# One ScalarE operation of 2048 columns for the hi part of a second-pass weight block, in place of two of 1024

## The chip, the cores and the metric

The kernel runs on one core of a Trainium2 chip. The metric is the device time of one launch in microseconds, as the median of several runs. The kernel before has a median of 2189.2 us over three runs (2186.03 to 2189.44).

## What is computed

One layer of an encoder over 512 tokens of width 2048, batch 1, all in float32: a normalisation, forgetting attention with 16 heads, a residual sum, a second normalisation and a SwiGLU feed-forward block of inner width 5632.

```python
def reference(x, ...):
    h = rmsnorm(x, mix_norm_g[0])
    x = x + forgetting_attention(h, fox_w_in[0], fox_b_f[0], fox_q_norm_g[0],
                                 fox_k_norm_g[0], fox_w_out[0])
    h = rmsnorm(x, ffn_norm_g[0])
    return x + swiglu(h, ffn_w_gate_up[0], ffn_w_down[0])

def swiglu(h, w_gu, w_down):
    gu = jnp.einsum('bsd,df->bsf', h, w_gu)
    gate, up = gu[..., :D_FF], gu[..., D_FF:]
    return jnp.einsum('bsf,fd->bsd', jax.nn.silu(gate) * up, w_down)
```

The change lies in the feed-forward block alone, in both of its matrix products (up: 2048 to 2 x 5632, down: 5632 to 2048).

## The kernel before

Every engine has its own program, written out by hand in one block each (`block.sync`, `block.gpsimd`, `block.tensor`, `block.scalar`, `block.vector`). An engine works through its program in order, and waits for others by semaphores that count up. Attention takes the first 834 us of the profiled execution, and the feed-forward block the rest.

**Products in hi and lo parts.** A float32 operand is split in two: ScalarE copies it in the narrower type that TensorE multiplies fast (`f_hi`), VectorE subtracts the copy from the original (`f_lo`), and TensorE makes each product of three matmuls (lines 723 to 725).

**Seven products in place of eight.** The feed-forward products are made by a Strassen-like scheme on 2 x 2 blocks, with seven block products. A *round* r makes one group of output columns (512 columns of each of two column blocks). Rounds 0 to 10 make the up product, rounds 11 to 16 the down product. A round has two *passes*, g = 0 and g = 1, and each pass has one *unit* per pair of blocks along the inner dimension: eight units in rounds 0 to 12, seven in rounds 13 to 16. All units, 264 of them, are numbered through by n (`UNITS`); so rounds 0 to 12 have 16 units each, and the second pass of round 2 is units 40 to 47.

- A first-pass unit loads three weight blocks of 128 x 512 (its raw buffer `f_raw` has four places of this size), and TensorE makes three products, 18 matmuls.
- A second-pass unit loads four blocks. VectorE turns them, in place, into four sums by three operations: t1 (line 1350, 1024 columns, gives places 0 and 1), then t2 (line 1355, gives place 3), then t3 (line 1357, gives place 2). Each adds one to the semaphore `t_step`; each of the later two waits for the one before. TensorE makes four products, 24 matmuls.

**The steps of a unit.** SyncE issues the load of unit n when TensorE is through with unit n - 4, since `f_raw` has four buffers. VectorE makes t1, t2, t3 of unit n + 2 while TensorE is in unit n. ScalarE makes `f_hi` of unit n + 2 (function `weights_hi`), which also waits for `unit_done`, that is until TensorE is through with unit n - 1, since `f_hi` has three buffers. For a second-pass unit it does so in two halves: line 1010 makes places 0 and 1 and waits for the first count of `t_step` only, and `weights_hi_rest`, line 1014, makes places 2 and 3 and waits for the third. VectorE then makes `f_lo` of the whole unit in one operation (`weights_lo`, line 1344), which waits for as many counts of `f_hi_done` as `HI_COUNT[n]` says. TensorE waits for `f_lo_done` at the start of each unit, and for nothing else in most.

**The order on VectorE.** In its iteration n of a second pass, VectorE issues t1(n + 2), then f_lo(n + 1), then t2(n + 2) and t3(n + 2). In two iterations of a round ("meeting": the last but one of the first pass, and the first of the second) f_lo comes ahead of t1. At the end of the first pass it reads product 2 out of PSUM (`read_p2`, line 1363, in the down rounds `add_p2_p3`, lines 1423 and 1428), at the end of the second the other products. In rounds 10 to 16 it also makes the lo parts of stored activations for the down product (`down_forms_lo`, line 1414), in many units at the end of the iteration.

**The order on ScalarE.** Beside `f_hi` it reads product 1 (`read_p1`, line 1027) and in the up rounds product 3 (`read_p3`, line 1034) out of PSUM at the last unit of the first pass. TensorE may write product 6 of the second pass only after product 1 has been read, and product 4 only after product 3 has been read; these are the second and the fourth product of the first second-pass unit.

## Time and profile before

| | |
|---|---|
| median of three runs | 2189.2 us (2186.03 to 2189.44) |
| profiled execution | 2189.52 us |
| its span | 2187.8 us |
| TensorE busy | 2129.5 us, 97% of the span |
| VectorE busy | 1524.6 us, 70% |
| ScalarE busy | 915.4 us, 42% |
| mean granted TensorE clock | 0.992 of full speed |

The span is the time from the first to the last instruction that was profiled; 1.7 us of the profiled execution lie outside it. Busy times of different engines overlap. A matmul of TensorE is recorded with 0.39 us, but the next one starts 0.23 us after it, as they are pipelined. On VectorE and ScalarE an operation that follows another without a wait starts some 0.1 us before the recorded end of the one before.

### The profile page before, as it was taken

The page shows a single profiled execution, that of the slowest core. Times are in us where ns is not written, and L with a number is a line of the kernel's source. Part 1 is how long each engine was busy: PE and PEld are TensorE (multiplying, and loading weights), DVE is VectorE, ACT ScalarE, POOL GpSimd, SP SyncE. Part 2 cuts the span into 40 slices and gives each one's busy share as a digit, 9 for nine tenths or more (in the row PEclk, how much of TensorE's full clock was granted, in tenths as well). Part 3 has the DMA queues.
Part 4 walks back from the last instruction along what each step waited for, and adds up shares of the span by engine and source line. Part 5 has one row for each costly group of instructions (what it writes and reads, how often), then busy time and mean ns, then how long its engine had stood idle before and what let it go on. Part 6 is the DMA issues. An engine that isn't in the chain of part 4 may idle for free.

```text
span 2187.8 us, 27845 instructions
## 1 busy us (share of the span) xinstructions
PE 2129.5 (97%) x10404; PEld 1852.7 (85%) x10404; DVE 1524.6 (70%) x2103; ACT 915.4 (42%) x1225; POOL 183.8 (8%) x356
## 2 busy tenths in 40 slices
PE   9999999999999999999999999999999989999997
PEld 8999999999998887888888888888887777777786
DVE  4544444444464445987888888788798888898888
ACT  5433333333343334444444444444445534444432
POOL 0322213222230000000000000000000001000000
PEclk9999999999999999999999999999999999999999
DMA  6332333333343335566566566567668757757755
GB/s 181 88 92 82 88 85 90 85 89 81 92 144 135 116 106 163 178 226 220 179 222 226 177 219 229 190 207 228 193 207 280 261 201 270 236 177 250 234 175 178
DMA packets 258331, 376.30 MB, mean 172 GB/s; under 512 B 15762, under 2 KB 114100, under 8 KB 257220
## 3 DMA queue, kind: packets, MB, share of 16 engines
q1 hardware_dynamic: 254864, 354.90, 51.6%
q10 hardware_dynamic: 3380, 20.21, 2.2%
q8 instruction: 58, 0.95, 0.2%
q14 instruction: 29, 0.24, 0.0%
HBM read 346.45 MB, written 28.61 MB: 171 GB/s over the span
## 4 chain that ended last, share of the span: by engine, by line
PE 83%; DVE 9%; DMA 6%; issue 1%; SPq 1%; POOL 0%; ACT 0%; DVEq 0%; POOLq 0%; ACTq 0%
PE gemm L522 11%; PE gemm L524 11%; PE gemm L523 11%; PE gemm L723 8%; PE gemm L725 8%; PE gemm L724 8%; PE aux L723 7%; PE aux L725 7%; PE aux L724 6%; DVE f_lo L1344 4%; DMA f_raw<-in_ffn_w_gate_up 3%; DMA f_raw<-in_ffn_w_down 2%; DVE f_raw L1350 2%; PE aux L523 1%; PE aux L524 1%; PE aux L522 1%
## 5 line engine op out<-in xcount | busy, mean ns | idle before, releaser
L1344 DVE TENSOR_TENSOR f_lo<-f_raw,f_hi 128x2048 fp32r<-128x2048 f32 (+1 forms) x264 | 534.2, 2030 | 63.9 <-ACT f_hi L1007 51.4
L522 PE MATMUL gemm<-w_hi,act_t 128*128 128x384 f32 (+2 forms) x1280 | 450.6, 352 | 1.6 <-DVE w_lo L1123 1.6
L524 PE MATMUL gemm<-w_hi,act_t 128*128 128x384 f32 (+2 forms) x1280 | 444.0, 347 | 0.0
L523 PE MATMUL gemm<-w_lo,act_t 128*128 128x384 f32 (+2 forms) x1280 | 443.9, 347 | 0.0
L723 PE MATMUL gemm<-f_hi,a_form 128*128 128x512 f32 x1056 | 412.4, 391 | 0.4 <-DVE rows L1428 0.4
L724 PE MATMUL gemm<-f_lo,a_form 128*128 128x512 f32 x1056 | 411.7, 390 | 0.0
L725 PE MATMUL gemm<-f_hi,a_form 128*128 128x512 f32 x1056 | 411.3, 389 | 0.0
L723 PE MATMUL aux<-f_hi,a_form 128*128 128x512 f32 x792 | 318.3, 402 | 42.8 <-DVE f_lo L1344 42.8
L725 PE MATMUL aux<-f_hi,a_form 128*128 128x512 f32 x792 | 312.2, 394 | 0.0
L724 PE MATMUL aux<-f_lo,a_form 128*128 128x512 f32 x792 | 311.9, 394 | 0.0
L1123 DVE TENSOR_TENSOR w_lo<-w_raw,w_hi 128x768 fp32r<-128x768 f32 (+1 forms) x160 | 160.8, 1009 | 208.5 <-ACT w_hi L818 208.5
L1007 ACT ACTIVATE f_hi<-f_raw 128x1536 fp32r<-128x1536 f32 x132 | 196.0, 1487 | 253.8 <-PE gemm L725 93.2
L522 PEld LDWEIGHTS gemm<-w_hi,act_t 128*128 128x128 f32 x1280 | 241.0, 188 | 12.4 <-issue 2.0
L523 PEld LDWEIGHTS gemm<-w_lo,act_t 128*128 128x128 f32 x1280 | 241.0, 188 | 10.4
L524 PEld LDWEIGHTS gemm<-w_hi,act_t 128*128 128x128 f32 x1280 | 240.8, 188 | 10.1
L723 PEld LDWEIGHTS gemm<-f_hi,a_form 128*128 128x128 f32 x1056 | 199.1, 189 | 42.6 <-DVE rows L1428 0.8
L724 PEld LDWEIGHTS gemm<-f_lo,a_form 128*128 128x128 f32 x1056 | 199.0, 188 | 41.6
L725 PEld LDWEIGHTS gemm<-f_hi,a_form 128*128 128x128 f32 x1056 | 198.8, 188 | 41.7
L1010 ACT ACTIVATE f_hi<-f_raw 128x1024 fp32r<-128x1024 f32 x132 | 139.9, 1060 | 222.2 <-DVE f_raw L1350 218.2
L1014 ACT ACTIVATE f_hi<-f_raw 128x1024 fp32r<-128x1024 f32 x132 | 140.2, 1062 | 210.5 <-DVE f_raw L1357 210.5
L723 PEld LDWEIGHTS aux<-f_hi,a_form 128*128 128x128 f32 x792 | 150.3, 190 | 88.2 <-DVE f_lo L1344 58.5
L818 ACT ACTIVATE w_hi<-w_raw 128x768 fp32r<-128x768 f32 (+1 forms) x160 | 136.4, 883 | 187.8 <-PE gemm L524 187.8
(161 smaller groups left out, 2143.0 us busy)
## 6 DMA issues: line engine op xcount, KB each, us to landing
f_raw<-in_ffn_w_gate_up SPq DMA_DIRECT2D x264, 512.0 KB, 4.2
f_raw<-in_ffn_w_down SPq DMA_DIRECT2D x132, 512.0 KB, 4.8
w_raw<-in_fox_w_in SPq DMA_DIRECT2D x192, 256.0 KB, 3.4
f_raw<-in_ffn_w_gate_up SPq DMA_DIRECT2D x88, 256.0 KB, 4.0
w_raw<-in_fox_w_out SPq DMA_DIRECT2D x16, 1024.0 KB, 5.1
a_raw<-forms_scratch SPq DMA_DIRECT2D x22, 512.0 KB, 6.3
f_raw<-in_ffn_w_down SPq DMA_DIRECT2D x44, 256.0 KB, 4.8
forms_scratch<-fa_a ACTq DMA_DIRECT2D x11, 896.0 KB, 6.3
```

Of the source, the lines that this page charges most:

```text
L522: mm(out, a_hi, b_hi, start=first, stop=False)
L523: mm(out, a_hi, b_lo, start=False, stop=False)
L524: return mm(out, a_lo, b_hi, start=False, stop=last)
L723: mm(banks[t][:], st_hi, hi, start=j == 0, stop=False)
L724: mm(banks[t][:], st_hi, lo, start=False, stop=False)
L725: i = mm(banks[t][:], st_lo, hi, start=False, stop=j == ROUND_K[r] - 1)
L818: a.activation(w_hi[:, j % 2, k, 0:width], w_raw[:, j % 2, k, 0:width], ACT.Copy)\
L1007: a.activation(f_hi[:, n % 3, 0:3], f_raw[:, n % 4, 0:3], ACT.Copy).then_inc(f_hi_done, 1)
L1010: a.activation(f_hi[:, n % 3, 0:2], f_raw[:, n % 4, 0:2], ACT.Copy).then_inc(f_hi_done, 1)
L1014: a.activation(f_hi[:, n % 3, 2:4], f_raw[:, n % 4, 2:4], ACT.Copy).then_inc(f_hi_done, 1)
L1123: v.tensor_tensor(w_lo[:, j % 2, k, 0:width], w_raw[:, j % 2, k, 0:width], f32(w_hi[:, j % 2, k, 0:width]), ALU.subtract).then_inc(w_lo_do ...
L1344: v.tensor_tensor(f_lo[:, n % 4, 0:3 + g], f_raw[:, n % 4, 0:3 + g], f32(f_hi[:, n % 3, 0:3 + g]), ALU.subtract).then_inc(f_lo_done, 1)
```

## The change

`weights_hi` makes the four places of a second-pass unit in one operation of 2048 columns. It waits for the third count of `t_step`, as the second half did. `weights_hi_rest` is gone, and with it one count of `f_hi_done` for each of the 132 second-pass units. At the last unit of a first pass ScalarE now reads product 1 ahead of `weights_hi`, and product 3 behind it. Nothing is changed in the code of SyncE, GpSimd, VectorE and TensorE, except for the number that VectorE's f_lo waits for.

```diff
@@ -82,7 +82,7 @@
         in_slot[n % 4] += 32
         LANDED.append(in_slot[n % 4])
         T_COUNT.append(ts)
-        his += 1 + g_
+        his += 1
         ts += g_
         HI_COUNT.append(his)
     A11, A12, S4, S2, S1, S3, A22, A21 = range(8)
@@ -1006,12 +1006,8 @@
                     act.wait_ge(f_ld[n % 4], LANDED[n])
                     a.activation(f_hi[:, n % 3, 0:3], f_raw[:, n % 4, 0:3], ACT.Copy).then_inc(f_hi_done, 1)
                 else:
-                    act.wait_ge(t_step, 3 * T_COUNT[n] + 1)
-                    a.activation(f_hi[:, n % 3, 0:2], f_raw[:, n % 4, 0:2], ACT.Copy).then_inc(f_hi_done, 1)
-
-            def weights_hi_rest(n):
-                act.wait_ge(t_step, 3 * T_COUNT[n] + 3)
-                a.activation(f_hi[:, n % 3, 2:4], f_raw[:, n % 4, 2:4], ACT.Copy).then_inc(f_hi_done, 1)
+                    act.wait_ge(t_step, 3 * T_COUNT[n] + 3)
+                    a.activation(f_hi[:, n % 3], f_raw[:, n % 4], ACT.Copy).then_inc(f_hi_done, 1)
 
             def read_p1(r):
                 dst = u_two if r < R_DOWN else junk_act
@@ -1076,14 +1072,12 @@
                 if g == 0:
                     if j == 0 and hidden:
                         gate_bot(r - 1)
+                if g == 0 and last:
+                    read_p1(r)
                 if n + 2 < NU:
                     weights_hi(n + 2)
-                if g == 0 and last:
-                    read_p1(r)
-                    if r < R_DOWN:
-                        read_p3(r)
-                if n + 2 < NU and UNITS[n + 2][1] == 1:
-                    weights_hi_rest(n + 2)
+                if g == 0 and last and r < R_DOWN:
+                    read_p3(r)
                 if g == 0:
                     if r == 0 and j == 1:
                         form_read(6, fa_a)
```


On ScalarE in an up round, from the hi part of the first unit of a second pass on (it is made in the last but one unit of the first pass). Here `f_hi` rows of 1024 columns are the halves, `forms_scratch` is a store that ScalarE issues, `u_two<-aux` is the reading of product 1 and `h_top<-gemm` that of product 3. Before, as far as the fourth unit's first half:

```order
L1010 ACTIVATE f_hi<-f_raw 128x1024 [waits t_step,unit_done]
L1014 ACTIVATE f_hi<-f_raw 128x1024 [waits t_step]
L1062 DMA forms_scratch<-fa_b 128x1792 [waits form_done]
L1010 ACTIVATE f_hi<-f_raw 128x1024 [waits t_step,unit_done]
L1027 ACTIVATE u_two<-aux 128x512 [waits product_done,forms_stored0]
L1027 ACTIVATE u_two<-aux 128x512 [waits product_done]
L1034 ACTIVATE h_top<-gemm 128x512 [waits product_done]
L1034 ACTIVATE h_top<-gemm 128x512 [waits unit_done]
L1014 ACTIVATE f_hi<-f_raw 128x1024 [waits t_step]
L1010 ACTIVATE f_hi<-f_raw 128x1024 [waits t_step,unit_done]
L1014 ACTIVATE f_hi<-f_raw 128x1024 [waits t_step]
L1010 ACTIVATE f_hi<-f_raw 128x1024 [waits t_step,unit_done]
```


And after, the whole second pass:

```order
L1010 ACTIVATE f_hi<-f_raw 128x2048 [waits t_step,unit_done]
L1058 DMA forms_scratch<-fa_b 128x1792 [waits form_done]
L1023 ACTIVATE u_two<-aux 128x512 [waits product_done,forms_stored0]
L1023 ACTIVATE u_two<-aux 128x512 [waits product_done]
L1010 ACTIVATE f_hi<-f_raw 128x2048 [waits t_step,unit_done]
L1030 ACTIVATE h_top<-gemm 128x512 [waits product_done]
L1030 ACTIVATE h_top<-gemm 128x512 [waits unit_done]
L1010 ACTIVATE f_hi<-f_raw 128x2048 [waits t_step,unit_done] x3
L1037 ACTIVATE c_one<-c_one,rms_x 128x512 [waits p2_read] x2
L1010 ACTIVATE f_hi<-f_raw 128x2048 [waits t_step,unit_done] x3
```


The reading of product 1 has moved ahead of the hi part of the second unit, and that of product 3 stands behind all of it; before, both stood between its halves. From there on each unit has one row in place of two.

On VectorE the same place in the program after the change, from the reading of product 2 (`c_one<-gemm`) on, in which `f_lo` rows wait for ScalarE, and the row of 1024 columns is t1, those of 512 columns t2 and t3 (line numbers are six lower than before):

```order
L1357 TENSOR_TENSOR c_one<-gemm,u_two 128x512 [waits product_done,p1_read] x2
L1338 TENSOR_TENSOR f_lo<-f_raw,f_hi 128x2048 [waits f_hi_done]
L1344 TENSOR_TENSOR f_raw<-f_raw 128x1024 [waits f_loaded2]
L1349 TENSOR_TENSOR f_raw<-f_raw 128x512 [waits t_step]
L1351 TENSOR_TENSOR f_raw<-f_raw 128x512 [waits t_step]
L1344 TENSOR_TENSOR f_raw<-f_raw 128x1024 [waits f_loaded3]
L1338 TENSOR_TENSOR f_lo<-f_raw,f_hi 128x2048 [waits f_hi_done]
```


Nothing moved here: t2 and t3 of a unit, t1 of the next, then f_lo of the first of the two.

## Rows read from the trace of the kernel before

**Rows 1.** the page: span, and busy us (share of the span) xinstructions.

```profile
span 2187.8 us, 27845 instructions
...
PE 2129.5 (97%) x10404; PEld 1852.7 (85%) x10404; DVE 1524.6 (70%) x2103; ACT 915.4 (42%) x1225; POOL 183.8 (8%) x356
```

**Rows 2.** busy us of PE PEld DVE ACT POOL, PEclk, DMA share, GB/s.

```profile
900.00:1700.00 800.00, 789.55 (x3549) 651.62 (x3549) 668.13 (x670) 357.11 (x368) 0.00 (x0) 1.00 0.65 213
1700.00:2188.00 488.00, 449.98 (x1919) 362.77 (x1917) 418.29 (x403) 200.00 (x189) 12.36 (x4) 0.97 0.67 220
```

**Rows 3.** who waited for whom: us in total, times, longest.

```profile
ACT f_hi L1014 <- DVE f_raw L1357: 210.5, 132, 2.5
...
PE aux L723 <- DVE f_lo L1344: 42.8, 35, 5.2
...
DVE f_lo L1344 <- ACT f_hi L1014: 12.4, 11, 1.1
```

**Rows 4.** ScalarE groups by shape: xcount, busy us, mean ns, idle before.

```profile
L1014 ACT ACTIVATE f_hi<-f_raw 128x1024 fp32r<-128x1024 f32 x132 | 140.2, 1062 | 210.5 <-DVE f_raw L1357 210.5
...
L963 ACT ACTIVATE a_form<-fa_x 128x1792 fp32r<-128x1792 f32 x6 | 10.2, 1696 | 6.1 <-PE gemm L524 4.7 <-DVE fa_x L1286 1.4
```

**Rows 5.** VectorE in time, round 2: start us, us, line, what, [idle].

```profile
1029.46 0.69 DVE L1357 TENSOR_TENSOR f_raw<-f_raw 128x512 f32<-128x512 f32 x1
...
1031.94 2.28 DVE L1344 TENSOR_TENSOR f_lo<-f_raw,f_hi 128x2048 fp32r<-128x2048 f32 x1
...
1036.68 2.29 DVE L1344 TENSOR_TENSOR f_lo<-f_raw,f_hi 128x2048 fp32r<-128x2048 f32 x1
1038.89 1.22 DVE L1350 TENSOR_TENSOR f_raw<-f_raw 128x1024 f32<-128x1024 f32 x1
1040.14 0.69 DVE L1355 TENSOR_TENSOR f_raw<-f_raw 128x512 f32<-128x512 f32 x1
1040.87 0.69 DVE L1357 TENSOR_TENSOR f_raw<-f_raw 128x512 f32<-128x512 f32 x1
1041.48 1.22 DVE L1350 TENSOR_TENSOR f_raw<-f_raw 128x1024 f32<-128x1024 f32 x1
1042.69 2.29 DVE L1344 TENSOR_TENSOR f_lo<-f_raw,f_hi 128x2048 fp32r<-128x2048 f32 x1
```

**Rows 6.** ScalarE in time, second half of unit 42.

```profile
1041.60 1.06 ACT L1014 ACTIVATE f_hi<-f_raw 128x1024 fp32r<-128x1024 f32 x1 [0.33 <-DVE f_raw L1357]
```

**Rows 7.** TensorE in time, first matmuls of units 40, 41, 42, 47.

```profile
1034.28 0.50 PE L723 MATMUL aux<-f_hi,a_form 128*128 128x512 f32 x1 [1.31 <-DVE f_lo L1344]
...
1039.86 0.39 PE L723 MATMUL aux<-f_hi,a_form 128*128 128x512 f32 x1
...
1045.30 0.39 PE L723 MATMUL aux<-f_hi,a_form 128*128 128x512 f32 x1
...
1072.49 0.39 PE L723 MATMUL aux<-f_hi,a_form 128*128 128x512 f32 x1
```

**Rows 8.** VectorE, start of the second pass of round 5.

```profile
1267.49 0.69 DVE L1357 TENSOR_TENSOR f_raw<-f_raw 128x512 f32<-128x512 f32 x1
...
1269.31 2.29 DVE L1344 TENSOR_TENSOR f_lo<-f_raw,f_hi 128x2048 fp32r<-128x2048 f32 x1
```

**Rows 9.** VectorE, second pass of round 10, units 174 and 175.

```profile
1701.14 0.69 DVE L1357 TENSOR_TENSOR f_raw<-f_raw 128x512 f32<-128x512 f32 x1
1701.75 1.22 DVE L1414 TENSOR_TENSOR a_form<-a_raw,a_form 128x1024 fp32r<-128x1024 f32 x1
1702.97 2.29 DVE L1344 TENSOR_TENSOR f_lo<-f_raw,f_hi 128x2048 fp32r<-128x2048 f32 x1
```

**Rows 10.** TensorE after a long wait, and two stretches by engine.

```profile
1840.64 0.50 PE L723 MATMUL aux<-f_hi,a_form 128*128 128x512 f32 x1 [1.91 <-DVE f_lo L1344]
...
1842.00:1846.00 4.00, 4.00 (x12) 3.14 (x11) 4.00 (x5) 1.74 (x2) 0.00 (x0) 0.58 0.54 185
...
1034.00:1040.00 6.00, 5.72 (x25) 4.76 (x26) 5.96 (x7) 2.19 (x4) 0.00 (x0) 1.00 0.91 357
```


## The prediction

> **What bounds the kernel now.** I read the page first: TensorE is busy for 97% of the span [rows 1]. The windows say where it is not: in the up rounds it is idle for some 10 of 800 us, at the full granted clock, in the down rounds for 38 of 488 us [rows 2]. The list of waits says why: nearly all of it, 42.8 us in 35 places, is waiting for f_lo, the last link of the chain load, sums, hi, lo [rows 3]. So TensorE sets the time, and the chain through VectorE and ScalarE stands close behind it. The same list has ScalarE idle for 210.5 us ahead of its second halves, one time in each of the 132 second-pass units, and VectorE idle for only 12.4 us because of them [rows 3]. What counts is therefore not how busy ScalarE is, but how soon after t3 the last hi part is there.
>
> **What it is now, in one unit.** Take unit 42 in round 2. t3 starts at 1040.87 and ends at 1041.56. ScalarE starts the second half at 1041.60 and ends at 1042.66 [rows 6]. VectorE meanwhile makes t1 of unit 43 from 1041.48, and starts f_lo at 1042.69 [rows 5]: 1.13 after the end of t3, without a gap. The second half, 1.06, hides behind t1, which takes 1.21 of VectorE's time. From one f_lo to the next VectorE needs 2.21 (f_lo, from 1036.68 to 1038.89), 1.42 (t2 and t3, 1040.14 to 1041.56) and 1.13, which is 4.76. TensorE needs 5.44 for a unit (1039.86 to 1045.30) [rows 7], so VectorE gains 0.68 a unit and recovers from each late start.
>
> **The new operation.** It cannot start before t3 ends, and makes 2048 columns. The trace has no copy of that size: 1024 columns take 1.062, 1792 columns 1.696 [rows 4], so one column costs 0.83 ns and 2048 columns about 1.91, from either row. Bounds: 1.89, if it is as if back to back, and 2.12, two halves without any saving. I take 1.92. With 0.04 to start after t3 and 0.03 until VectorE starts, as now [rows 5, 6], f_lo comes 1.99 after the end of t3 in place of 1.13. **Each second-pass unit is exposed to 0.86 more on VectorE**, in which VectorE idles: behind the waiting f_lo stand t2 and t3 of the next unit, and so the next hi part. It is a loop, and its length goes from 4.76 to 2.21 + 1.42 + 1.99 = 5.62, which is longer than TensorE's 5.44. That decides the case.
>
> **What one up round pays.** From f_lo of unit 40 to f_lo of unit 47 there are seven steps. Six take 5.62. The one from unit 41 to 42 has t1 of unit 42 in the chain too (1038.89 to 1040.14, 1.25 [rows 5], the "meeting" order), so 6.87; the sum is 40.59. TensorE took 1072.49 - 1034.28 = 38.21 for these seven units [rows 7], and it follows f_lo by 0.05 in either case. So unit 47 starts 2.38 later, and takes 0.14 longer, as each unit does that starts after a wait (unit 40 took 5.58, 1034.28 to 1039.86). **2.52 a round.** How it builds up: f_lo of unit 41, 0.86 late, just uses up its lead (it ended at 1038.97, and TensorE came at 1039.86); unit 42 is 1.72 late with a lead of 0.31, so TensorE waits 1.4 there; then 0.18 in each unit. Ten up rounds (0 to 9): 25.2.
>
> **The start of the pass.** f_lo of the first unit comes after t1 of the second, which waits for its load. In round 2 it started 1031.94 - 1030.15 = 1.79 after the end of t3 [rows 5], so 0.20 is exposed; in round 5 it was 1269.31 - 1268.18 = 1.13 [rows 8], so 0.86. Six of the ten rounds are under 1.99, and their differences add up to 2.8. VectorE's lateness at the end of a pass is not carried on: it then waits for TensorE's products. The loads are issued when TensorE leaves a unit, so they move with it.
>
> **Round 10 and the down rounds.** Here VectorE often has other work between t3 and f_lo that covers the new operation. In unit 175, t3 ends at 1701.83 and one L1414 fills the 1.14 until f_lo [rows 9]: exposed by 0.85, since t1 is missing there. Where L1414 and t1 both stand between (0.87 + 1.14 or 1.14 + 1.14), or two pairs of PSUM reads (2.3), nothing is exposed or 0.1. On the other hand TensorE waits for f_lo already in many units, so that what is exposed counts at once. I carried the lateness through unit by unit with the same 1.99, letting a load move with TensorE. It gives 3.0 for round 10 (0.86 exposed in four of its first six steps and in the last; VectorE then enters round 11 late), and 1.9, 1.6, 1.2, 0.9, 1.1 and 1.4 for rounds 11 to 16, together 11.1. From below this is 0 if all of it is covered, from above 7 x 2.5 = 17.6.
>
> **The moved readings.** Product 1 is read ahead of a hi part that has to wait for t3 anyway, so it costs nothing, and it comes earlier for VectorE's reading of product 2, which follows t3 in VectorE's own order. Product 3 now comes behind the hi part of the second unit. In round 2 that hi part would end at 1035.76 + 0.04 + 1.92 = 1037.7, and the first of the two readings (0.6 each) at 1038.3; TensorE wants the bank three products (4.08) after unit 40 starts at 1034.5, at 1038.6. Hidden by 0.3, the least cover in the change. If it fails, up to 0.5 is added in each of eleven rounds, but TensorE then waits less in unit 42, so I count 0. ScalarE saves 132 x 0.2 = 27 us of work, all of it idle time already.
>
> **The sum.** 25.2 + 2.8 + 11.1 = 39.1 on the profiled execution of 2189.5, so 2228.6. The median is 0.3 lower: **2228.3**.
>
> **Two rules of the Trainium skill.** By its page "VectorE: DVE Perf Modes", section "The TRN2 errata — SBUF-src ops pay a fixed extra latency per instruction", one large tile pays that latency once, and small ones pay it each time; this speaks for the change. The durations agree: two halves take 2.12, one is to take 1.92 [rows 4]. By the page "Perfetto Trace Analysis", section "Optimizing Scalar/DVE Operations", larger operations help "if the engine is saturated", and engines that are not but cause bubbles on others should rather have their operations broken up; this speaks against it. By the first alone the kernel would gain or stay; by the second it loses. ScalarE's 210.5 us of idle time [rows 3] bear out the second.
>
> **The rivals.**
> *The clock falls.* New waits of 1.4 to 1.6 on TensorE might bring its slower level. After a wait of 1.91 the granted clock was 0.58 in the stretch 1842 to 1846, half of full speed for most of it, and 12 matmuls started in 4.0 us, where 17.6 do at 5.44 for 24 [rows 10]: 1.3 lost. But after unit 40's wait of 1.31 [rows 7] it stayed at 1.00 [rows 10]. If it fell once in each of 14 second passes, the 1.3 would be set off against the 0.9 of waiting that follows in the pass: 14 x 0.4 = 6, so 2234; fully paid, 14 x 1.3 = 18, so 2246. Chance 0.1.
> *Lateness does not add up.* If the loop is shorter than reckoned, by 0.18 or more, only the wait in unit 42 is left, about 1.4 a round: 14 + 2 + 6 = 22, so 2211. Every link of it stands in the trace [rows 5, 6], except for the 1.92. Chance 0.07.
> *Two halves without saving.* 2.12 makes the loop 5.82: seven times 0.2 more in each of 14 passes, 20 us, less in the down rounds: 2245. Chance 0.03; the longer copies speak against it [rows 4].
> *Not slower: ScalarE was the limit.* Then 27 us of ScalarE work saved, and one semaphore count less, would shorten the chain: at most 2162. It decides if ScalarE is still busy with earlier work when t3 ends, since it would then be released sooner. In round 2 it had been idle for 0.33 when t3 of unit 42 ended [rows 6], and it idles ahead of all 132 second halves. Chance 0.02. That VectorE's idle time is covered after all and nothing changes: 0.02.
>
> **How the numbers follow.** The forecast case has 0.76, with its own range 2219 to 2237 (the 11.1 between 0 and 17.6, the operation from 1.89). The range is drawn to 2215 to 2243, which takes in the clock case and most of the slower copy. A measurement of this kernel can tell some 0.2% (4 us) from no change: faster 0.02, same 0.02, slower 0.96.
>
> **What would show it.** In the profile after: f_hi of 2048 columns at 1.92; VectorE idle for ScalarE's f_hi in nearly all second-pass units of the up rounds, about 0.75 each, in sum near 80 in place of 12.4; TensorE waiting for f_lo for about 80 in place of 42.8, with 1.4 to 1.6 in the third unit of each second pass and 0.04 to 0.2 in those behind it; an up round of 81.6 in place of 79; no wait of TensorE at the fourth product of a pass's first unit. I am wrong if f_lo starts less than 1.8 after the end of t3, or if second-pass units of the up rounds still follow each other at 5.44, or if granted clock falls in the up rounds.

## The result, and the profile after

| | before | after |
|---|---|---|
| median | 2188.62 us (2186.03 to 2189.44, 4 runs) | 2235.69 us (2232.53 to 2235.93, 4 runs) |
| profiled execution's span | 2187.8 us | 2234.1 us |

The ratio is 1.021, with a 95% interval of 1.0195 to 1.0225. The kernel became slower by 47 us in the medians and by 46.3 in the profiled executions. The forecast was 2228.3, in a range of 2215 to 2243.

The page, beside [rows 1]. Columns: busy us, share of the span, instructions.

```profile
span 2234.1 us, 27713 instructions
...
PE 2150.4 (96%) x10404; PEld 1843.2 (83%) x10404; DVE 1521.6 (68%) x2103; ACT 889.8 (40%) x1093; POOL 184.3 (8%) x356
```

ScalarE has 132 instructions fewer and 25.6 us less to do, and the span is longer. TensorE's busy time has grown by 21 although it does the same 10404 matmuls. A small wait hides there: a matmul is recorded with 0.39 us while the next one starts 0.23 after it, so a matmul that comes 0.22 late adds 0.16 to "busy" and only 0.06 to idle time. TensorE's share says less here than the distance between the starts of its units.

The same two kinds of stretch as [rows 2] (busy us of PE, PEld, DVE, ACT, POOL, then granted clock, DMA share, GB/s):

```profile
900.00:1700.00 800.00, 776.17 (x3422) 622.54 (x3420) 635.88 (x643) 326.37 (x274) 0.00 (x0) 1.00 0.62 202
1700.00:2234.00 534.00, 486.13 (x2056) 384.96 (x2056) 450.56 (x432) 209.06 (x159) 12.48 (x4) 0.98 0.66 218
```

In the up rounds TensorE starts 3422 matmuls in 800 us in place of 3549, at a granted clock of 1.00 in both. So the clock is not what slows them.

The list of waits, beside [rows 3] (us in total, times, longest):

```profile
ACT f_hi L1010 <- DVE f_raw L1351: 529.1, 131, 11.0
...
PEld aux L723 <- DVE f_lo L1338: 116.9, 135, 5.9
DVE f_lo L1338 <- ACT f_hi L1010: 96.5, 96, 2.3
...
PE aux L723 <- DVE f_lo L1338: 65.8, 48, 5.5
```

ScalarE now waits 529 us for t3, since nothing else is left for it to do in between, and that costs nothing. The line that costs is the third: VectorE stood 12.4 us for a hi part before, and 96.5 now, in 96 places. TensorE's wait for f_lo appears in two rows. A long wait stands in both, at the matmul (42.8 us before, 65.8 now) and at TensorE's weight load for it (58.5 in 38 places before, 116.9 in 135 now). A short one stands at the weight load alone: there were 3 such places before, and there are 87 now. The two rows are two readings of one wait, so they are not to be added.

Of the chain that ended last, the page gives the shares by engine:

```profile
PE 70%; DVE 18%; DMA 5%; ACT 5%; issue 1%; SPq 1%; POOL 0%; ACTq 0%; DVEq 0%
```

Before, TensorE had 83% of that chain and VectorE 9%. The chain has moved over to VectorE's loop.

ScalarE's group by shape, beside [rows 4] (count, busy us, mean ns; idle before, and who ended it):

```profile
L1010 ACT ACTIVATE f_hi<-f_raw 128x2048 fp32r<-128x2048 f32 x132 | 253.3, 1919 | 534.1 <-DVE f_raw L1351 529.1 <-PE gemm L725 5.0
```

The operation takes 1919 ns, as forecast (1.92).

Now VectorE in round 2, beside [rows 5]. Columns: start, us, engine, line, operation, and in brackets the idle time before it and who ended it. Here L1351 is t3, L1344 t1, L1338 f_lo.

```profile
1047.98 0.69 DVE L1351 TENSOR_TENSOR f_raw<-f_raw 128x512 f32<-128x512 f32 x1
1048.59 1.22 DVE L1344 TENSOR_TENSOR f_raw<-f_raw 128x1024 f32<-128x1024 f32 x1
1050.72 2.29 DVE L1338 TENSOR_TENSOR f_lo<-f_raw,f_hi 128x2048 fp32r<-128x2048 f32 x1 [0.91 <-ACT f_hi L1010]
...
1056.38 2.29 DVE L1338 TENSOR_TENSOR f_lo<-f_raw,f_hi 128x2048 fp32r<-128x2048 f32 x1 [0.91 <-ACT f_hi L1010]
```

ScalarE in the same stretch:

```profile
1041.84 1.92 ACT L1010 ACTIVATE f_hi<-f_raw 128x2048 fp32r<-128x2048 f32 x1 [2.77 <-DVE f_raw L1351]
1043.67 1.07 ACT L1030 ACTIVATE h_top<-gemm 128x512 f32<-128x512 f32 x2
1048.77 1.92 ACT L1010 ACTIVATE f_hi<-f_raw 128x2048 fp32r<-128x2048 f32 x1 [4.04 <-DVE f_raw L1351]
```

And TensorE's first matmuls of units 40, 41, 42, 43 and 47, beside [rows 7], with the weight load of unit 43, which shows its short wait:

```profile
1040.48 0.50 PE L723 MATMUL aux<-f_hi,a_form 128*128 128x512 f32 x1 [1.47 <-DVE f_lo L1338]
...
1046.14 0.50 PE L723 MATMUL aux<-f_hi,a_form 128*128 128x512 f32 x1
...
1053.07 0.50 PE L723 MATMUL aux<-f_hi,a_form 128*128 128x512 f32 x1 [1.19 <-DVE f_lo L1338]
...
1058.73 0.19 PEld L723 LDWEIGHTS aux<-f_hi,a_form 128*128 128x128 f32 x1 [0.33 <-DVE f_lo L1338]
1058.73 0.50 PE L723 MATMUL aux<-f_hi,a_form 128*128 128x512 f32 x1
...
1081.39 0.50 PE L723 MATMUL aux<-f_hi,a_form 128*128 128x512 f32 x1
```

Read them together. t3 of unit 42 starts at 1047.98 and ends at 1048.67. ScalarE starts at 1048.77 and takes 1.92. VectorE is through with t1 of unit 43 at 1049.81, stands idle for 0.91, and starts f_lo at 1050.72, which is 2.05 after the end of t3. TensorE had waited 1.19 for exactly this and starts unit 42 at 1053.07, when f_lo ends. The next f_lo comes 5.66 later (1056.38), and so does the next unit (1058.73). The units followed each other at 5.44 before.

Where the 46.3 us lie, from the starts of TensorE's units after against before:

| stretch | forecast | measured |
|---|---|---|
| attention | 0 | 0.4 |
| up rounds 0 to 9, second passes | 25.2 | 29.2 |
| up rounds 0 to 9, starts of the passes | 2.8 | 2.0 |
| round 10, to the first units of round 11 | 3.0 | 4.8 |
| down rounds 11 to 16 | 8.1 | 10.0 |
| sum | 39.1 | 46.4 |

The sum is 46.4 and not 46.3 by rounding. In round 2 one second pass goes like this: unit 40 to unit 47 took 38.21 and takes 40.91, so 2.70, and unit 47 itself takes 0.13 longer: 2.83. Rounds 1, 6 and 9 lose 0.3 more. In each of them the operation of one unit (25, 111 and 153) started 0.37 us after t3 and not 0.09, though ScalarE was idle. Unit 25, t3 and then ScalarE's operation:

```profile
958.21 0.69 DVE L1351 TENSOR_TENSOR f_raw<-f_raw 128x512 f32<-128x512 f32 x1
...
959.27 1.92 ACT L1010 ACTIVATE f_hi<-f_raw 128x2048 fp32r<-128x2048 f32 x1 [3.06 <-DVE f_raw L1351]
```

The same three units are late in experiment 4, which has the same program for ScalarE, and none is in experiment 3. So this goes with the program and not with chance; what causes it was not tested.

### The profile page after: what moved, and what is told of

The parts are those of the page before. It is cut to its first block, busy times and chain, and to the rows that moved or that the text cites. A ratio compares the mean times of both kernels' runs of the same rounds, so it can differ in the third digit from the quotient of the medians.

```text
span 2234.1 us, 27713 instructions
## 1 busy us (share of the span) xinstructions
PE 2150.4 (96%) x10404; PEld 1843.2 (83%) x10404; DVE 1521.6 (68%) x2103; ACT 889.8 (40%) x1093; POOL 184.3 (8%) x356
## 4 chain that ended last, share of the span: by engine, by line
PE 70%; DVE 18%; DMA 5%; ACT 5%; issue 1%; SPq 1%; POOL 0%; ACTq 0%; DVEq 0%
PE gemm L522 11%; PE gemm L524 11%; PE gemm L523 11%; DVE f_lo L1338 9%; PE gemm L725 6%; PE gemm L724 6%; PE gemm L723 6%; PE aux L723 5%; ACT f_hi L1010 5%; PE aux L725 5%; PE aux L724 5%; DMA f_raw<-in_ffn_w_gate_up 3%; DVE f_raw L1344 2%; DVE f_raw L1351 2%; DVE f_raw L1349 2%; DMA f_raw<-in_ffn_w_down 1%
## 5 line engine op out<-in xcount | busy, mean ns | idle before, releaser
L1338 DVE TENSOR_TENSOR f_lo<-f_raw,f_hi 128x2048 fp32r<-128x2048 f32 (+1 forms) x264 | 533.9, 2028 | 146.3 <-ACT f_hi L1010 96.5
L1010 ACT ACTIVATE f_hi<-f_raw 128x2048 fp32r<-128x2048 f32 x132 | 253.3, 1919 | 534.1 <-DVE f_raw L1351 529.1
L723 PE MATMUL aux<-f_hi,a_form 128*128 128x512 f32 x792 | 329.5, 416 | 66.3 <-DVE f_lo L1338 65.8
L725 PE MATMUL aux<-f_hi,a_form 128*128 128x512 f32 x792 | 312.6, 395 | 0.0
L723 PEld LDWEIGHTS aux<-f_hi,a_form 128*128 128x128 f32 x792 | 150.2, 190 | 143.8 <-DVE f_lo L1338 116.9
L1344 DVE TENSOR_TENSOR f_raw<-f_raw 128x1024 f32<-128x1024 f32 x132 | 161.0, 1220 | 60.9 <-DMA f_raw<-in_ffn_w_gate_up 37.8
```

What stands on the lines that cost most here:

```text
L723: mm(banks[t][:], st_hi, hi, start=j == 0, stop=False)
L725: i = mm(banks[t][:], st_lo, hi, start=False, stop=j == ROUND_K[r] - 1)
L1010: a.activation(f_hi[:, n % 3], f_raw[:, n % 4], ACT.Copy).then_inc(f_hi_done, 1)
L1338: v.tensor_tensor(f_lo[:, n % 4, 0:3 + g], f_raw[:, n % 4, 0:3 + g], f32(f_hi[:, n % 3, 0:3 + g]), ALU.subtract).then_inc(f_lo_done, 1)
L1344: v.tensor_tensor(f[:, 0:2], f[:, 0:2], f[:, 1:4:2], ALU.add).then_inc(t_step, 1)
```

## The experiments

The theory: the new operation starts only when t3 has ended and takes 1.92, of which t1 hides 1.1. The rest lengthens VectorE's loop from one f_lo to the next from 4.76 to over TensorE's 5.44. It has three links that can be pulled apart: the halves themselves, the moved readings of products 1 and 3, and the order of VectorE's work that decides how much is covered. What was new in the profile was 2.05 from t3 to f_lo, where 1.99 was forecast. The operation started 0.09 to 0.10 after the end of t3 (in 129 of 132 units), while the second half of before started 0.03 to 0.04 after it (in all 132). The rivals are lost clock, the moved readings, and the longer operation as such, whenever it starts.

Each kernel was timed beside the kernel before on the same chip; that one's median was 2187.88 for the first four, 2189.85 for the next four, 2192.22 for the last.

| kernel | median us | ratio (95%) | t3 to f_lo | units of up rounds apart | paid by a second pass of an up round |
|---|---|---|---|---|---|
| changed kernel | 2235.7 | 1.021 (1.0195 to 1.0225) | 2.05 | 5.66 | 2.9 |
| halves, readings as after | 2190.0 | 1.0006 (0.9996 to 1.0015) | 1.13 | 5.44 | 0 |
| two halves, both after t3 | 2243.3 | 1.025 (1.0232 to 1.0267) | 2.13 | 5.75 | 3.45 |
| the waits in the other order | 2228.3 | 1.0173 (1.0158 to 1.0188) | 1.99 | 5.61 | 2.4 |
| VectorE's order changed | 2217.6 | 1.0121 (1.0098 to 1.0144) | 2.05 | 5.44 | 1.3 |
| 512 columns early, 1536 late | 2202.0 | 1.005 (1.0034 to 1.0066) | 1.56 | 5.44 | 0.8 |
| both readings behind the hi part | 2256.3 | 1.029 (1.0268 to 1.0311) | 2.05 | 5.66 | 4.6 |
| one operation in down rounds only | 2202.5 | 1.005 (1.0034 to 1.0065) | 1.13 | 5.44 | 0 |
| both orders changed | 2213.0 | 1.0096 (1.0074 to 1.0118) | 1.99 | 5.44 | 1.3 |
| before, the waits in the other order | 2189.5 | 0.9994 (0.998 to 1.0007) | 1.13 | 5.44 | 0 |

**1. The halves again, with the readings where the change puts them.** This undoes one part of the change and leaves the other.

```diff
                 else:
-                    act.wait_ge(t_step, 3 * T_COUNT[n] + 3)
-                    a.activation(f_hi[:, n % 3], f_raw[:, n % 4], ACT.Copy).then_inc(f_hi_done, 1)
+                    act.wait_ge(t_step, 3 * T_COUNT[n] + 1)
+                    a.activation(f_hi[:, n % 3, 0:2], f_raw[:, n % 4, 0:2], ACT.Copy).then_inc(f_hi_done, 1)
+
+            def weights_hi_rest(n):
+                act.wait_ge(t_step, 3 * T_COUNT[n] + 3)
+                a.activation(f_hi[:, n % 3, 2:4], f_raw[:, n % 4, 2:4], ACT.Copy).then_inc(f_hi_done, 1)
...
                     read_p3(r)
+                if n + 2 < NU and UNITS[n + 2][1] == 1:
+                    weights_hi_rest(n + 2)
```

> The changed kernel with the hi part of a second-pass unit in two halves again (the first after t1, the second after t3), but with the reading of product 1 ahead of it and product 3 behind its first half, as the change has it. Theory (the wait for t3 with the whole copy behind it is all of the cost): the time of before, 2189 within 3 us, f_lo again 1.13 us after the end of t3. Rival (part of the cost comes from product 3 being read later or product 1 earlier): 2195 to 2210, with TensorE waiting at the fourth product of a pass's first unit.

It gave 2189.97 and a ratio of 1.0006. VectorE, where t3 is now L1357, t1 L1350 and f_lo L1344:

```profile
1041.24 0.69 DVE L1357 TENSOR_TENSOR f_raw<-f_raw 128x512 f32<-128x512 f32 x1
1041.85 1.22 DVE L1350 TENSOR_TENSOR f_raw<-f_raw 128x1024 f32<-128x1024 f32 x1
1043.06 2.29 DVE L1344 TENSOR_TENSOR f_lo<-f_raw,f_hi 128x2048 fp32r<-128x2048 f32 x1
...
1047.81 2.29 DVE L1344 TENSOR_TENSOR f_lo<-f_raw,f_hi 128x2048 fp32r<-128x2048 f32 x1
```

f_lo follows t1 without a gap, 1.13 after the end of t3 (1041.93), and the next one comes 4.75 later. Beside two halves the moved readings cost nothing: the whole loss comes with the one operation. The rival of the readings falls, as far as it stands by itself.

**2. Two halves, both after t3.** This separates "one operation" from "starts after t3".

```diff
                     act.wait_ge(t_step, 3 * T_COUNT[n] + 3)
-                    a.activation(f_hi[:, n % 3], f_raw[:, n % 4], ACT.Copy).then_inc(f_hi_done, 1)
+                    a.activation(f_hi[:, n % 3, 0:2], f_raw[:, n % 4, 0:2], ACT.Copy)
+                    a.activation(f_hi[:, n % 3, 2:4], f_raw[:, n % 4, 2:4], ACT.Copy).then_inc(f_hi_done, 1)
```

> The changed kernel with two operations of 1024 columns in place of the one of 2048, but both after t3 and with one signal. Theory (what costs is that the copy starts after t3): no part of the loss comes back, and the two operations take 0.1 us longer than the one, so the step from f_lo to f_lo in an up round goes from 5.66 to 5.76 and the time to about 2244 (2240 to 2248). Rival (one large operation is itself the trouble, its size or its single signal): back towards 2189.

It gave 2243.28, 7.6 more than the changed kernel. ScalarE, unit 42:

```profile
1050.57 1.07 ACT L1010 ACTIVATE f_hi<-f_raw 128x1024 fp32r<-128x1024 f32 x1 [4.04 <-DVE f_raw L1352]
1051.53 1.04 ACT L1011 ACTIVATE f_hi<-f_raw 128x1024 fp32r<-128x1024 f32 x1
```

The second starts 0.96 after the first, so the pair takes 2.00, 0.08 more than the one operation, and the loop is 5.75 in place of 5.66, as expected. So the one operation is cheaper as such. It is slower than before only because nothing of it can start before t3: the early half was made while VectorE did t2 and t3.

**3. The two waits in the other order.** The hi part waits for two semaphores, t_step and unit_done. In the trace of the changed kernel the one written later in the code, t_step, stands as an instruction of its own on ScalarE's queue ahead of the operation, and the operation itself carries the other. Here t_step is written first.

```diff
                 r, g, j = UNITS[n]
+                if g == 1:
+                    act.wait_ge(t_step, 3 * T_COUNT[n] + 3)
                 if n < 2:
...
                 else:
-                    act.wait_ge(t_step, 3 * T_COUNT[n] + 3)
                     a.activation(f_hi[:, n % 3], f_raw[:, n % 4], ACT.Copy).then_inc(f_hi_done, 1)
```

> The changed kernel with ScalarE's two waits ahead of the 2048-column operation in the other order, the one for t3 first and the one for TensorE's unit second. In the trace of the changed kernel the later one stands as an instruction of its own on the sequencer and the operation starts 0.09 us after t3, where the second half of before, with one wait, started 0.03 to 0.04 after it. Theory (the separate instruction adds 0.05 to each step, which is the larger part of what the prediction missed): start 0.04 after t3, step 5.61, 0.35 us less in each up round, 3.5 to 5 us less in all, 2231. Rival (0.09 belongs to the size or to the number of waits, whatever their order): 2235.7 and a start after 0.09.

It gave 2228.32, 7.4 less than the changed kernel, or 6.6 less with each against its own kernel before. Expected were 3.5 to 5 less. First VectorE's t3 (now L1352), then ScalarE's operation, then two of VectorE's f_lo (L1339):

```profile
1048.22 0.69 DVE L1352 TENSOR_TENSOR f_raw<-f_raw 128x512 f32<-128x512 f32 x1
...
1048.95 1.92 ACT L1011 ACTIVATE f_hi<-f_raw 128x2048 fp32r<-128x2048 f32 x1 [3.98 <-DVE f_raw L1352]
...
1050.90 2.29 DVE L1339 TENSOR_TENSOR f_lo<-f_raw,f_hi 128x2048 fp32r<-128x2048 f32 x1 [0.85 <-ACT f_hi L1011]
...
1056.51 2.29 DVE L1339 TENSOR_TENSOR f_lo<-f_raw,f_hi 128x2048 fp32r<-128x2048 f32 x1 [0.85 <-ACT f_hi L1011]
```

t3 ends at 1048.91 and ScalarE starts at 1048.95; over the kernel it is 0.03 to 0.04 after t3 in all 132 units, in place of 0.09. f_lo comes 1.99 after t3, and the loop is 5.61 where the changed kernel has 5.66. By stages it pays 25.9 in the up rounds, 4.8 in round 10 and 8.2 in the down rounds, against 31.2, 4.8 and 10.0. Of the 5.3 in the up rounds some 4.3 are 0.4 in each of ten second passes, which is the 0.06 seven times over, and some 0.8 are the three starts after 0.37 us, which are gone here. So 0.06 us in the order of two waits is worth 5 to 7 us of 2236, since it is added to a loop that sets the pace. By the page "Perfetto Trace Analysis" of the Trainium skill, section "Identifying Dependency Chains", an instruction that waits on several engines may have separate EventSemaphore instructions ahead of it. That is what the trace shows; the price of 0.06 and that the order written decides are from these runs.

**4. Cover from VectorE's own work.** t1 and t2 of the next unit but one go ahead of f_lo, and t3 behind it, so that ScalarE's operation runs beside f_lo too. In the first unit of a second pass, where f_lo came ahead of t1, t1 goes first.

```diff
                 v.tensor_tensor(f[:, 3], f[:, 0], f[:, 3], ALU.add).then_inc(t_step, 1)
+
+            def sums_t3(n):
+                f = f_raw[:, n % 4]
                 dve.wait_ge(t_step, 3 * T_COUNT[n] + 2)
...
-                meeting = (g == 0 and j == ROUND_K[r] - 2) or (g == 1 and j == 0)
+                meeting = g == 0 and j == ROUND_K[r] - 2
                 if sums and not meeting:
                     sums_t1_t3(n + 2)
+                    if g == 1 and j > 0:
+                        sums_t2_t4(n + 2)
...
                 if sums:
-                    sums_t2_t4(n + 2)
+                    if not (g == 1 and j > 0):
+                        sums_t2_t4(n + 2)
+                    sums_t3(n + 2)
```

> The changed kernel with another order on VectorE in second passes: t1 and t2 of the next unit but one now both stand between t3 of a unit and its f_lo (before it was t1 alone, and nothing for the second unit of a pass), so that 1.9 to 2.3 us of VectorE's own work cover the 2.0 of the copy. Theory (a loop longer than TensorE's 5.44 us is what adds up): the loop is 4.98, second-pass units of an up round from the fourth on follow each other at 5.44 again, what is left is about 0.9 a round from f_lo coming later once, and the time is about 2203 (2195 to 2210). Rival (the loss is in ScalarE's copy itself or in TensorE's waits, whatever covers them): 2230 or more.

It gave 2217.6: faster than the changed kernel by 18, but 15 more than expected. VectorE in round 2, t1 L1344, t2 L1349, t3 L1354, f_lo L1338:

```profile
1042.08 1.23 DVE L1344 TENSOR_TENSOR f_raw<-f_raw 128x1024 f32<-128x1024 f32 x1 [0.59 <-DMA f_raw<-in_ffn_w_gate_up]
1043.22 2.28 DVE L1338 TENSOR_TENSOR f_lo<-f_raw,f_hi 128x2048 fp32r<-128x2048 f32 x1
...
1046.14 0.69 DVE L1354 TENSOR_TENSOR f_raw<-f_raw 128x512 f32<-128x512 f32 x1
1046.75 1.22 DVE L1344 TENSOR_TENSOR f_raw<-f_raw 128x1024 f32<-128x1024 f32 x1
1048.00 0.69 DVE L1349 TENSOR_TENSOR f_raw<-f_raw 128x512 f32<-128x512 f32 x1
1048.88 2.29 DVE L1338 TENSOR_TENSOR f_lo<-f_raw,f_hi 128x2048 fp32r<-128x2048 f32 x1 [0.18 <-ACT f_hi L1010]
...
1053.82 2.29 DVE L1338 TENSOR_TENSOR f_lo<-f_raw,f_hi 128x2048 fp32r<-128x2048 f32 x1 [0.18 <-ACT f_hi L1010]
```

The loop is what was expected: f_lo follows f_lo at 4.94, ScalarE is waited for only 0.18, and from the fourth unit on TensorE's units are 5.44 apart again. What was missed is the first row. t1 of unit 42, now ahead of f_lo of unit 41, waits 0.59 for its load, which was issued from 1033.76 on, 8.3 before t1 could start, and holds that f_lo back. TensorE loses 0.7 to 1.1 there in eight of the ten up rounds and 0.25 in the other two, and 0.4 in two more steps. In round 10 the same wait came with a longer stop of TensorE. This order takes the operation out of the loop, and puts a load in its place. It did not come back to the time of before.

**5. A quarter early.** How much has to start early? 512 columns after t1, 1536 after t3; the rest is as in experiment 1.

```diff
-                    act.wait_ge(t_step, 3 * T_COUNT[n] + 3)
-                    a.activation(f_hi[:, n % 3], f_raw[:, n % 4], ACT.Copy).then_inc(f_hi_done, 1)
+                    act.wait_ge(t_step, 3 * T_COUNT[n] + 1)
+                    a.activation(f_hi[:, n % 3, 0:1], f_raw[:, n % 4, 0:1], ACT.Copy).then_inc(f_hi_done, 1)
+
+            def weights_hi_rest(n):
+                act.wait_ge(t_step, 3 * T_COUNT[n] + 3)
+                a.activation(f_hi[:, n % 3, 1:4], f_raw[:, n % 4, 1:4], ACT.Copy).then_inc(f_hi_done, 1)
```

> Two operations again, cut elsewhere: 512 columns (place 0) after t1 and 1536 columns (places 1 to 3) after t3, product 1 read ahead and product 3 between them. 1536 columns with one wait take 0.03 + 1.49 + 0.03 = 1.55 us from the end of t3 to f_lo, so 0.42 of it is not hidden. Theory (what counts is whether VectorE's loop is longer than TensorE's 5.44): the loop is 5.18, so lateness does not add up; only the third unit of a pass pays, some 0.5 to 0.7 an up round, and the time is about 2198 (2194 to 2203), a fifth of the change's loss for half of its added wait. Rival (the loss is in proportion to what stands behind t3): half of 47, 2212.

It gave 2202.02. ScalarE's late part, then VectorE's f_lo (L1344):

```profile
1050.74 1.49 ACT L1014 ACTIVATE f_hi<-f_raw 128x1536 fp32r<-128x1536 f32 x1 [3.17 <-DVE f_raw L1357]
...
1047.09 2.29 DVE L1344 TENSOR_TENSOR f_lo<-f_raw,f_hi 128x2048 fp32r<-128x2048 f32 x1 [0.42 <-ACT f_hi L1014]
...
1052.27 2.29 DVE L1344 TENSOR_TENSOR f_lo<-f_raw,f_hi 128x2048 fp32r<-128x2048 f32 x1 [0.42 <-ACT f_hi L1014]
```

VectorE is idle 0.42 in each step, and the loop is 5.18 (1047.09 to 1052.27), still under 5.44. So the lateness does not add up: TensorE pays 0.6 once, in the third unit of the pass, and 0.7 in nine of the ten second passes in all. Expected were 2198, and the theory of this size of loss holds within 4 us. The four lengths of the loop, 4.75, 5.18, 5.61 and 5.66, cost 2, 12, 40 and 47 us in the medians, each against its own kernel before (experiments 1, 5 and 3, and the changed kernel); the 2 is not clear of noise. The first 0.42 of idle time of VectorE in a unit costs 10 to 12, the next 0.43 costs 28, because with it the loop passes 5.44.

**6. Both readings behind the hi part.** In the changed kernel product 1 is read ahead of the hi part. If it stood behind it, the new wait would reach PSUM.

```diff
-                if g == 0 and last:
-                    read_p1(r)
                 if n + 2 < NU:
                     weights_hi(n + 2)
-                if g == 0 and last and r < R_DOWN:
-                    read_p3(r)
+                if g == 0 and last:
+                    read_p1(r)
+                    if r < R_DOWN:
+                        read_p3(r)
```

> The changed kernel (one operation of 2048 columns) with the readings of product 1 and of product 3 both behind the hi part of the second unit, where they stood before, in place of product 1 ahead of it. Theory (the move ahead is what keeps TensorE from waiting at the second product of a pass's first unit): product 1 would be read at about 3.3 us after that unit's start, where TensorE wants the bank after 1.4 us; some 2 us more in each up round and 1 in the down rounds, 2260 to 2272. Rival (product 1 has slack enough in any place): 2235.7.

It gave 2256.32, 21 more than the changed kernel, a little less than the 2260 to 2272 that were expected. TensorE's first matmul of unit 40 and, behind it, the first of the unit's second product; between them ScalarE's readings of product 1:

```profile
1044.51 0.50 PE L723 MATMUL aux<-f_hi,a_form 128*128 128x512 f32 x1 [1.18 <-DVE f_lo L1338]
...
1047.69 0.58 ACT L1023 ACTIVATE u_two<-aux 128x512 f32<-128x512 f32 x1
...
1048.33 0.50 PE L723 MATMUL aux<-f_hi,a_form 128*128 128x512 f32 x1 [2.15 <-ACT u_two L1023]
```

TensorE waits 2.15 within the unit, for its bank. In this kernel the two levels of the clock are seen too: in round 1 the same wait of 2.17 (at 964.34) was followed by this stretch, with the granted clock as the last but two figure:

```profile
966.00:970.00 4.00, 4.00 (x13) 3.12 (x13) 3.93 (x4) 0.00 (x0) 0.00 (x0) 0.65 0.00 0
```

It is 0.65 there, a mean over time at both of the two levels of 1.2 and 2.4 GHz, while in round 2 a wait of 2.15 brought no fall. Six of the eleven up rounds (0 to 10) had such a fall, and they lost 4.05 in the first unit of the second pass in place of 2.4. The move of the reading ahead of the hi part is thus a part of the change that pays: without it the change would have cost 66 us (against 2189.85 beside it) and not 47.

**7. The one operation in the down rounds only.** It tests the part of the sum that was carried through.

```diff
-        his += 1
+        his += 1 + (g_ if r_ < R_DOWN else 0)
...
+                    if r >= R_DOWN:
+                        act.wait_ge(t_step, 3 * T_COUNT[n] + 3)
+                        a.activation(f_hi[:, n % 3], f_raw[:, n % 4], ACT.Copy).then_inc(f_hi_done, 1)
+                    else:
```

The lines behind the last `else` are those of experiment 1.

> One operation of 2048 columns in the six down rounds alone, two halves in the eleven up rounds, product 1 read ahead in all. Theory (in the trace of the changed kernel 36 of the 46 us stand by the start of the down rounds): 2188 + 10 = 2198 (2195 to 2202), with third units of the up rounds without a wait. Rival (part of the down rounds' loss is brought along from the up rounds or comes from how their loads fall): within 4 us of 2188, or over 2204.

It gave 2202.48. The down rounds lost 11.2, round 10 lost 0.8, and the up rounds nothing. In the changed kernel the down rounds lost 10.0, after 36 us of lateness in the rounds before them. So their loss stands by itself and is not an heir of the up rounds. The median is 4 us above the 2198 that were expected: 2 of them lie in the kernel before, which had 2189.85 beside it and not 2188. In the profiled execution 1.6 lie in attention, which the edit does not touch.

**8. Both orders changed**, that is experiments 3 and 4 together; the edit is the sum of the two.

> The changed kernel with VectorE's order of the covered run and ScalarE's two waits in the other order. In the covered run t1 of the third unit waited for its load and held back f_lo of the second, 0.95 us in each up round; that stays. Theory: the f_lo behind t1 and t2 starts 1.98 to 2.0 after t3 in place of 2.05, which no longer adds up, since the loop is under 5.44 in either case: 0.1 to 0.2 less in each pass, 2215 (2211 to 2219). Rival (each 0.05 counts in each unit, as it does in the loop of 5.66): 2210 or less.

It gave 2212.97, 4.6 under experiment 4, which is not clear of noise, as the two intervals overlap. With the loop under 5.44 the 0.06 is worth nothing more in the up rounds (14.9 there, against 15.0). The profiled executions differ by 2.6 in the down rounds (4.6 against 7.2), and by 3.5 in round 10, where experiment 4 had a stop of 2.87 and a fall of the clock that this one did not have. That these are the price of the 0.06 is not shown.

**9. The kernel before with the waits of its first half in the other order.**

```diff
                 r, g, j = UNITS[n]
+                if g == 1:
+                    act.wait_ge(t_step, 3 * T_COUNT[n] + 1)
                 if n < 2:
...
-                    act.wait_ge(t_step, 3 * T_COUNT[n] + 1)
                     a.activation(f_hi[:, n % 3, 0:2], f_raw[:, n % 4, 0:2], ACT.Copy).then_inc(f_hi_done, 1)
```

> The kernel before, with ScalarE's two waits ahead of the first half (1024 columns, after t1) in the other order, the one for t1 first. Theory (a twentieth of a us counts only where it stands in a loop longer than TensorE's unit): the first half starts 0.04 after t1 in place of 0.09 to 0.10, and nothing else moves, within 2 us of before. Rival (fewer instructions of the sequencer near an operation help in themselves): 4 us or more faster than before, as the 7 us of the same edit on the changed kernel.

It gave 2189.49, a ratio of 0.9994. ScalarE's first half (L1011) of unit 42:

```profile
1040.84 1.06 ACT L1011 ACTIVATE f_hi<-f_raw 128x1024 fp32r<-128x1024 f32 x1 [3.49 <-DVE f_raw L1351]
```

Its t1 ended at 1040.81, so the half starts 0.03 behind it; in the kernel before, the same half started 0.09 to 0.10 behind t1 in 113 of 132 units. The 0.06 is there, and nothing of the time moves, as that half has slack. No version was found that beats the kernel before.

## Why the prediction was right, and where it was off

**The mechanism was right, link by link.** The new operation at 1.92 (1.919 measured); ScalarE had no work left when t3 ended (2.77 and 4.04 idle before the operation in the rows above); VectorE idle for ScalarE near 80 us (96.5, with 0.91 each in the rows above and not 0.75); 1.4 to 1.6 of waiting ahead of the third unit of a pass (unit 41 took 6.92 in place of 5.44, 1.48 more, of which the matmul's row shows 1.19); then a small loss in each unit behind it; an up round of 81.6 (82.6 in round 2, where it was 79.6); the clock at 1.00 in up rounds 0 to 9. TensorE's waiting for f_lo was forecast at 80 and reads 65.8 at the matmuls and 116.9 at the weight loads, so this sign could have been met or missed by the choice of the row. The stretch behind the 1.19 wait shows the last of these:

```profile
1053.00:1059.00 6.00, 5.93 (x25) 4.70 (x26) 5.06 (x6) 1.92 (x1) 0.00 (x0) 1.00 0.53 175
```

Of the three things that were to prove it wrong two did not come: f_lo comes 2.05 after t3 and not under 1.8, and the units are 5.66 apart and not 5.44. The third came once: the clock did not fall in up rounds 0 to 9, but it fell in round 10, which is an up round too and in which it had not fallen before. This cost 1.6 us there (below), and does not carry the 46.

**The step that was mis-sized is "0.04 to start after t3".** It was read off the second half of before, at L1014 [rows 6], which waits for one semaphore. The new operation waits for two, and starts 0.09 after t3. The trace of before held a row for that case: the first half, L1010, has two waits, and it started 0.09 to 0.10 after t1 (in 113 of 132 units). The prediction took the row of the operation with the same releaser, where it should have taken the one with the same waits. With 2.05 the loop is 5.68 by the prediction's own working, and 5.66 was measured, against 5.62 forecast. In round 2 the pass paid 0.09 in unit 40, 1.48 at the third unit, 0.22 or 0.23 in each of the five steps behind it and 0.13 in unit 47, which is 2.83; the forecast was 2.52, with 1.4 and 0.18. Experiment 3 takes this term away, and the three late starts with it, and lands on 2228.3, which is the forecast. That agreement has some luck in it, since its parts differ: 25.9 in the up rounds against 28.0 forecast, 4.8 against 3.0 in round 10, 8.2 against 8.1 in the down rounds.

**Round 10 was too low, 3.0 against 4.8.** It is 4.8 in experiment 3 too, so this is not the 0.06. Some of it may be scatter: experiments 1, 7 and 9, which have two halves in this round, differ from before by 0.2 to 0.8 there. VectorE at the start of that second pass (units 168 and 169), where L1344 is t1 of unit 169 and L1338 f_lo of unit 168:

```profile
1697.64 1.23 DVE L1344 TENSOR_TENSOR f_raw<-f_raw 128x1024 f32<-128x1024 f32 x1 [2.02 <-DMA f_raw<-in_ffn_w_gate_up]
1698.79 2.29 DVE L1338 TENSOR_TENSOR f_lo<-f_raw,f_hi 128x2048 fp32r<-128x2048 f32 x1
```

And the same t1 in the kernel before:

```profile
1664.41 1.23 DVE L1350 TENSOR_TENSOR f_raw<-f_raw 128x1024 f32<-128x1024 f32 x1 [0.22 <-DMA f_raw<-in_ffn_w_gate_up]
```

t1 waits for its load in both, 0.22 before and 2.02 now. SyncE issued this load at 1658.39 before and at 1689.91 after, right as TensorE left unit 165 (at 1658.20 and 1689.72). So it moved with TensorE, as the prediction had it; but t1 came 6.0 after the issue before and 7.7 after it now. f_lo of unit 168 was 4.03 behind t3, and TensorE waited 3.08:

```profile
1701.13 0.50 PE L723 MATMUL aux<-f_hi,a_form 128*128 128x512 f32 x1 [3.08 <-DVE f_lo L1338]
...
1702.00:1706.00 4.00, 4.00 (x12) 3.14 (x11) 3.16 (x4) 3.51 (x4) 0.00 (x0) 0.57 0.88 342
```

Behind that wait the granted clock was 0.57, and the unit took 7.19 in place of 5.59. A part came back in the next unit: unit 169 took 5.44, where it had taken 5.95, since unit 170 started without its wait of 0.35. The prediction kept each load's duration, and this one's grew by 1.7. In experiment 3 it was 8.2 from the issue to t1, but in experiments 2 and 6, where the operation starts as late, 6.4 and 6.0, so the late operation alone does not bring it. What made it longer was not tested.

**The starts of the passes.** 2.8 forecast, 2.0 measured: the price of a late f_lo was a little lower in some rounds (0.16 in round 2, forecast 0.20) and absent in others.

**The down rounds.** 8.1 forecast, 10.0 measured, and 8.2 with the waits turned around. Round by round it fits badly: rounds 12 to 16 lost 2.9, -1.0, 0.8, 1.8 and 3.3, where 1.6, 1.2, 0.9, 1.1 and 1.4 were forecast, and in round 13 the kernel before had a fall of the clock that the changed kernel did not have. Experiments 1 and 9, which cost nothing in the medians, were 3.2 and 2.4 shorter than before in these rounds of their profiled executions. So the sum is right to within that scatter, with luck in it, and the 1.8 between 10.0 and 8.2 is not shown to be the 0.06.

**The moved readings cost 0** beside two halves, as experiment 1 shows, and beside the one operation no wait of TensorE stands at the fourth product of a pass's first unit in any up round. The cover was about as thin as reckoned: in round 2 the two readings of product 3 start at 1043.67 and take 1.07, so the first ends about 0.6 later, at 1044.3, and TensorE wants the bank at 1040.48 + 4.08 = 1044.56 at the earliest. In rounds 1 and 9, with their late start of 0.37, it was 0.3 less.

**The rivals.** That the clock falls did not happen in up rounds 0 to 9, where 31 of the 46 us lie. Behind them there were falls after long waits, at units 168, 184, 206 and 257, where before had them at 184, 185, 200 and 215, as many as now; this does not make the difference. That lateness does not add up is refuted by the 5.66, and experiment 5 shows the kernel in which it is true. Two halves without saving stands refuted by the 1919 ns, and experiment 2 has its time, 2243 against the 2245 that it was priced at. That ScalarE was the limit is refuted by its 529 us of waiting. The forecast case's own range, 2219 to 2237, is some 2 us too high for its stated bounds: 2228.3 less 11.1 is 2217, even before a shorter operation is taken off, and 6.5 more is 2235. The stated range of 2215 to 2243 holds either way.

**Of the two rules of the Trainium skill** that the prediction weighed, the one of "Perfetto Trace Analysis", section "Optimizing Scalar/DVE Operations", decided: ScalarE was not saturated, and its operation broken up lets f_lo start sooner (experiment 1: 2190, changed kernel: 2236). That larger operations are cheaper is true too, 2.00 against 1.92, and worth 7.6 us in experiment 2, less than the 47.

## What to carry to other kernels

Before two operations are merged, write down the loop that they stand in, from one start of the waiting engine to the next, and compare it with the period of the engine that sets the pace. Under that period a longer step costs once per pass, above it the excess is paid in every unit. Price a step by a row with the same waits as it will have, not only the same releaser, and where an instruction waits for two semaphores, write the one that comes last in the first place.

## What the runs showed of the hardware

- An operation of ScalarE with two waits started 0.09 us after its releaser when the wait that came last was written second, and 0.03 when it was written first (experiments 3 and 9). An operation with one wait started after 0.03. Three operations with two waits started after 0.37 (units 25, 111 and 153 of the changed kernel and of experiment 4), for a cause that is open.
- The copy of 2048 columns took 1919 ns, 1536 columns 1.49 us, and 1024 columns 1.06; two of 1024 back to back took 2.00.
- After waits of about 2 us TensorE's granted clock sometimes fell and sometimes did not: experiment 6 had 0.65 after a wait of 2.17 in one round, and no fall after 2.15 in the next. The kernel before had one after 1.91 (unit 200), the changed kernel none after 3.26 (at 2109.9). After the waits of 1.2 to 1.8 in up rounds 0 to 9 of the changed kernel it stayed at 1.00.
- The load of unit 42 in experiment 4 took 8.3 us from its issue until t1 could start, as long as one and a half units of TensorE (5.44 each). It is a limit close behind the one that was studied.
